# Two edits to a one-core block kernel: a halved update in a triangular inverse, and a reordered start of a recurrence

## The reference

```
a_low = where(strict, beta * (k k^T) * decay, 0)
sol = triangular_solve(a_low + eye, [v * beta, k * beta * exp(G)])
```

```
u = u + mu[0] * (prev - u) + mu[1] * (nxt - u)
S = S * w + (S (-kk)) (kk * a)^T + v k^T;   y = S r
```

## Time and profile before

| | |
|---|---|
| median of 3 runs | 3051.03 us (3050.25 to 3051.47) |
| profiled execution, its own time | 3045.2 us |
| its span | 3043.4 us |
| PE busy | 97% of the span |
| DVE / ACT / POOL busy | 49% / 36% / 8% |
| mean granted PE clock | 0.992 |

### The profile page before, as it was taken

The page is one execution under the profiler, slowest core; times in us unless marked ns, Lnnn a source line. Parts: engine busy times, 40 slices in busy tenths (PEclk is TensorE's granted clock), DMA queues, the critical chain, the costliest instruction groups (busy, mean ns, idle before and its releaser), DMA issues.

```text
span 3043.4 us, 46816 instructions
## 1 busy us (share of the span) xinstructions
PE 2942.6 (97%) x21214; PEld 2427.2 (80%) x21214; DVE 1479.4 (49%) x1443; ACT 1092.8 (36%) x1186; POOL 234.0 (8%) x135
## 2 busy tenths in 40 slices
PE   8998899999999999999999999999999998999998
PEld 6777778888888788888878878788878887888886
DVE  6765553444355444443454444555675654644432
ACT  5554442222345832222342222442244432332222
POOL 1002110000100010000110000320001220000001
PEclk9999999999999999999999999999998999999999
DMA  3210022222322012223222223312230002222231
GB/s 142 83 60 2 2 83 97 97 97 107 108 86 92 33 70 97 97 97 108 106 83 97 97 98 110 105 63 83 81 109 5 3 5 115 88 93 97 96 110 69
DMA packets 44902, 249.29 MB, mean 82 GB/s; under 512 B 8444, under 2 KB 12284, under 8 KB 17185
## 3 DMA queue, kind: packets, MB, share of 16 engines
q1 hardware_dynamic: 43552, 242.11, 22.4%
q10 hardware_dynamic: 1152, 4.19, 0.3%
HBM read 237.90 MB, written 8.39 MB: 81 GB/s over the span
## 4 chain that ended last, share of the span: by engine, by line
PE 85%; DVE 8%; ACT 4%; issue 2%; POOL 1%; DMA 0%; SPq 0%; DVEq 0%; ACTq 0%; POOLq 0%
PE ps L588 68%; PE ps L2756 7%; PE ps L1407 2%; ACT whi L266 1%; PE ps L2344 1%; DVE wlo L272 1%; PE ps L2328 1%; DVE gdn_XX L1775 1%; PE ps L3800 1%; PE ps L3781 1%; PE ps L3812 0%; PE ps L2064 0%; PE ps L2943 0%; DVE rw_u L1041 0%; DVE gdn_conv L1041 0%
## 5 line engine op out<-in xcount | busy, mean ns | idle before, releaser
L272 DVE TENSOR_TENSOR wlo<-wraw,whi 128x2048 fp32r<-128x2048 f32 x210 | 486.5, 2317 | 940.4 <-ACT whi L266 940.3
L266 ACT ACTIVATE whi<-wraw 128x2048 fp32r<-128x2048 f32 x210 | 402.1, 1915 | 926.6 <-PE ps L588 926.5
L588 PE MATMUL ps<-ffn_xh,whi 128*128 128x512 f32 x1408 | 552.3, 392 | 3.6 <-DVE ffn_xl L389 2.1
L588 PE MATMUL ps<-ffn_xh,wlo 128*128 128x512 f32 x1408 | 551.7, 392 | 0.0
L588 PE MATMUL ps<-ffn_xl,whi 128*128 128x512 f32 x1408 | 548.2, 389 | 0.0
L588 PEld LDWEIGHTS ps<-ffn_xh,whi 128*128 128x128 f32 x1408 | 264.5, 188 | 60.6 <-DVE ffn_xl L389 2.5
L588 PEld LDWEIGHTS ps<-ffn_xl,whi 128*128 128x128 f32 x1408 | 264.3, 188 | 59.4 <-issue 0.7
L588 PEld LDWEIGHTS ps<-ffn_xh,wlo 128*128 128x128 f32 x1408 | 264.4, 188 | 57.6
L588 PE MATMUL ps<-ffn_uh,whi 128*128 128x512 f32 x704 | 276.5, 393 | 0.0
L588 PE MATMUL ps<-ffn_uh,wlo 128*128 128x512 f32 x704 | 275.5, 391 | 0.0
L588 PE MATMUL ps<-ffn_ul,whi 128*128 128x512 f32 x704 | 273.5, 388 | 0.0
(11 more groups left out here) (509 smaller groups left out, 4705.5 us busy)
## 6 DMA issues: line engine op xcount, KB each, us to landing
wraw<-in_weights SPq DMA_DIRECT2D x211, 1024.0 KB, 4.8
gates_kept<-gates_tmp ACTq DMA_DIRECT2D x8, 512.0 KB, 4.1
mix_gate<-gates_kept SPq DMA_DIRECT2D x8, 512.0 KB, 10.8
h<-in_x SPq DMA_DIRECT2D x4, 512.0 KB, 9.5
mix_y<-hz_kept SPq DMA_DIRECT2D x2, 1024.0 KB, 6.3
out<-out SPq DMA_DIRECT2D x4, 512.0 KB, 3.2
wraw<-in_weights SPq DMA_DIRECT2D x2, 512.0 KB, 7.9
ple_raw<-in_p SPq DMA_DIRECT2D x4, 256.0 KB, 5.1
```

The source lines that it names most:

```text
L266: c.nc.scalar.activation(c.whi[:, j % 2, :], c.wraw[:, j % 2, :], ACT.Copy).then_inc(c.hi_ready, 1)
L272: c.nc.vector.tensor_tensor(c.wlo[:, j % 2, :], c.wraw[:, j % 2, :], c.whi[:, j % 2, :].bitcast(F32), ALU.subtract).then_inc(c.lo_ready, 1)
L588: last = nc.tensor.matmul(pair[:, m, :], a, b, start=opens and n == 0 and wa + xa == 0, stop=closes and n == len(ks) - 1 and wa == 1)
```

## The change

1. **Halved update.** `pe_right` signals `Z0` behind the X half and `Z` behind the XT half. `dve_right` is two subtractions of 128x512 in place of one of 128x1024: X behind `Z0` (signal `X`), XT behind `Z` (signal `XX`). The next `pe_left` waits for `X`, the next `pe_right` for `XX`. `Y21` still waits for `XX`.
2. **Preparations ahead of the last eviction.** DVE's slots 17 to 28 of the first preparation go behind tile 6 in place of tile 7, so ahead of the last `pad`.
3. **Late taps of two tiles.** Tiles 6 and 7 both leave their DVE taps for later, and these run in stage 0 of the recurrence in slots 21, 23, 25 and 27, one tap (two instructions) in each, in place of slot 5.
4. **Other banks.** The recurrence's banks depend on the projection's last pair: here Y = 6, Z = (0, 1), F = (4, 5), A = 2, C = 3. PE waits at the start for the `pad` of tile 6 alone, and for that of tile 7 only ahead of stage 1.

```diff
-            self.V.plan([f"{self.name}.pad{q}"] + [f"{self.name}.tap{q}.{w}" for w in range(1, len(self.taps))])
+            self.V.plan([f"{self.name}.pad{q}"])
+            for of in (q,) if q < n - self.late else range(n - self.late, n) if q == n - 1 else ():
+                self.V.plan([f"{self.name}.tap{of}.{w}" for w in range(1, len(self.taps))])
...
-        if not (self.late and r == len(self.body) - 1):
-            self.dve_taps(dve, q)
+        if q < len(self.body) - self.late:
+            for w in range(1, len(self.taps)):
+                self.dve_tap(dve, q, w)
...
         if l:
-            pe.wait_ge(*self.at("XX", i - 1))
+            pe.wait_ge(*self.at("X", i - 1))
...
         if l == 0:
             pe.wait_ge(*self.at("attT", 2 * k + 1))
+        else:
+            pe.wait_ge(*self.at("XX", i - 1))
         for h in range(2):
             for n in range(NC):
-                self.both(lambda r: X[r, h * NC + n, :], lambda r: self.XX[r, 1, h, n, :], lambda r: self.Y[r, h, n, :])
+                last = self.both(lambda r: X[r, h * NC + n, :], lambda r: self.XX[r, 1, h, n, :], lambda r: self.Y[r, h, n, :])
+        last.then_inc(*self.done("Z0"))
...
-        dve.wait_ge(*self.at("Z", LV * k + l))
-        XX = self.XX[:, :, :, :, :].rearrange("p x h n t -> p x (h n t)")
-        self.c.nc.vector.tensor_tensor(XX, XX, self.bank(self.Z_BANK, 2), ALU.subtract).then_inc(*self.done("XX"))
+        for x, (made, done) in enumerate((("Z0", "X"), ("Z", "XX"))):
+            dve.wait_ge(*self.at(made, LV * k + l))
+            X = self.XX[:, x, :, :, :].rearrange("p h n t -> p (h n t)")
+            self.c.nc.vector.tensor_tensor(X, X, self.bank(self.Z_BANK + x), ALU.subtract).then_inc(*self.done(done))
...
-    Y_BANK, Z_BANK, F_BANK, A_BANK, C_BANK, MISC = 0, (1, 2), (3, 4), 5, 6, 7
+    BANKS = ((6, (2, 3), (4, 5), 0, 1, 7), (6, (0, 1), (4, 5), 2, 3, 7))
...
-        pe.wait_ge(*self.shift.free(len(RW_ORDER) - 1))
+        last = len(RW_ORDER) - 1
+        pe.wait_ge(*self.shift.free(last - 1))
         for k, build, step, prepare, finish in self.pairs():
+            if k == 1:
+                pe.wait_ge(*self.shift.free(last))
...
-        for s in {3: range(8), 4: range(8, 12), 5: range(12, 17), 7: range(17, SLOTS)}.get(r, ()):
+        for s in {3: range(8), 4: range(8, 12), 5: range(12, 17), 6: range(17, SLOTS)}.get(r, ()):
...
-                if k == 0 and s == 5:
-                    self.shift.dve_taps(dve, len(RW_ORDER) - 1)
+                if k == 0 and s in (21, 23, 25, 27):
+                    of, w = divmod((s - 21) // 2, 2)
+                    self.shift.dve_tap(dve, len(RW_ORDER) - 2 + of, 1 + w)
```

More of the change, by code:

```diff
@@ L959, in __init__ @@
     def __init__(self, c, name, n, norm, dst, padded, taps, pad, bias=None, func=None, conv=None, beside=(),
-                 beside_pe=(), held=0, first=True, dst_free=None, order=None, late=False):
+                 beside_pe=(), held=0, first=True, dst_free=None, order=None, late=0):
         self.late = late
@@ L1024, in dve_evac, with dve_tap @@
                                 ALU.mult).then_inc(*self.V.done(f"{name}.pad{q}"))
-        if not (self.late and r == len(self.body) - 1):
-            self.dve_taps(dve, q)
+        if q < len(self.body) - self.late:
+            for w in range(1, len(self.taps)):
+                self.dve_tap(dve, q, w)
         for b in self.beside:
             b.vector_beside(dve, r)
-    def dve_taps(self, dve, q):
+    def dve_tap(self, dve, q, w):
         nc, name = self.c.nc, self.name
[L1032 to L1043, removed]
+        if w == 1:
+            dve.wait_ge(*self.V.at(f"{name}.pad{q}"))
+            dve.wait_ge(*self.A.at(f"{name}.tap{q}"))
+        else:
+            dve.wait_ge(*self.V.at(f"{name}.tap{q}.{w - 1}"))
+        at, col = self.taps[w]
+        for m in range(2):
+            to = self.to(q, m)
+            last = nc.vector.scalar_tensor_tensor(to, self.padded[:, q % 2, m, at:at + T], col(2 * self.order[q] + m), to,
+                                                  ALU.mult, ALU.add)
+        last.then_inc(*self.V.done(f"{name}.tap{q}.{w}"))
 def vec_at(c, name):
@@ L1282, in __init__ @@
         self.sems, self.made = {}, {}
-        for engine, cycles in (("pe", ("rb", "rq", "rg", "kk tX Y21 X12", "qk", "Y", "Z", "tv", "tk", "kS", "vn", "dS", "o",
+        for engine, cycles in (("pe", ("rb", "rq", "rg", "kk tX Y21 X12", "qk", "Y", "Z0 Z", "tv", "tk", "kS", "vn", "dS", "o",
                                        "osum")),
                                ("act", ("eg", "Dx", "vT", "kdT", "Xc Y21c Xd X12c", "Yc", "VN", "oc osq", "oln", "ors hi")),
-                               ("dve", ("eye", "kb", "qn", "diff", "dm qd", "AT", "off XT0", "attT", "XX", "R", "S", "on og lo", "zero")),
+                               ("dve", ("eye", "kb", "qn", "diff", "dm qd", "AT", "off XT0", "attT", "X XX", "R", "S", "on og lo", "zero")),
                                ("pool", ("CT", "mc"))):
@@ L2560, in __init__ @@
         self.j_held = c.tile
+        self.Y_BANK, self.Z_BANK, self.F_BANK, self.A_BANK, self.C_BANK, self.MISC = self.BANKS[(c.groups - 1) % 2]
         put = lambda name, shape, at: c.at(f"rw_{name}", shape, at)
@@ L4065, in second_half @@
     shift = Taps(c, "rw_u", 8, norm, u, padded, taps, 1, held=2, first=False, dst_free=keep.free,
-                 order=RW_ORDER, late=True)
+                 order=RW_ORDER, late=2)
     shift.beside_sync = (keep,)
```

## The result

| | before | after |
|---|---|---|
| median of 4 runs beside each other | 3051.25 us (3050.25 to 3051.82) | 3026.4 us (3025.8 to 3027.51) |
| ratio, 95% interval | | 0.9932 [0.9919, 0.9945] |
| span of the profiled execution | 3043.4 us | 3024.8 us |
| mean granted PE clock in it | 0.992 | 0.994 |

The medians differ by 24.9 us, the two spans by 18.6 us. The ratio, taken at the 3051.0 us of the forecast, is 3030.3 us [3026.3, 3034.2]; the forecast was 3032 us.

A forecast was written before the change was run, and what follows sets the result against it. PE, busy 97% of the span, was taken as the bound, so only its idle and slow time could be won. 8.2 + 0.3 + 1.3 - 0.5 + 10.0 = 19.3 us off 3051.0 gave 3032 us; 8-in-10 range 3027 to 3043.

The forecast's parts named there:

- the clean one: Likeliest case: all terms arrive and the clock does not fall at the recurrence; 3032 us, own range 3028 to 3036, chance 0.50.
- Halved update: Delta rule's core, four stages: PE's waits for the subtraction shrink, winning 8.2 us, bounds 4 and 11.8.
- the losses that I charged for the fuller DVE: Delta rule's later stages: DVE's extra instruction loses waits of 1.4 and 0.33 us and adds 0.15 to 0.2 us.
- The start of the recurrence: Recurrence's start: PE no longer waits for the last pad, but LT limits the win to 0.3 us, bounds 0 and 1.7.
- the 1.7 us that PE wins come out as 0.2 to 0.35 us: Recurrence's start: POOL's mask product and DVE's L3178 wait for LT, which starts little earlier; 0.3 us taken.
- Taps out of slot 5: Recurrence's first right product: `ys` is ready ahead of need, so PE's idle time goes; 1.3 us won, bounds 1.0 and 1.3.
- Late taps in slots 21 to 27: Recurrence's stage 0: taps fit DVE's room, but a POOL mask product may overrun slot 21; 0.5 us charged, bounds 0 and 3.
- The clock: Recurrence from about 2297 us: with less PE idle time the stretch at 1.2 GHz goes, winning 10.0 us.
- The slow stretch stays: Rival, recurrence: the clock falls at 2297 all the same, so only 9.3 us are won; 3042 us, chance 0.20.
- The early fall: Rival, recurrence's start: the clock falls at about 2279 for 3 to 5 us; 3036 us, chance 0.18.
- The other side: Rival, recurrence: an early fall lasts, costing up to 14 us more; 3056 us, chance 0.05 shared with some wait unseen.
- The halves do nothing: Rival, delta rule: POOL's mask product or PE's order bounds left products, 2 to 4 us won; 3037 to 3047 us, chance 0.07.

The follow-up runs named there:

- e1: Kernel before with only the halved update of Inverse added, recurrence untouched: 3038.84 us, before beside it 3047.84 us.
- e8: Kernel after, unchanged, run again in a later set: 3029.94 us, before beside it 3047.78 us, ratio 0.9943.
- e12: Kernel after, unchanged, run a third time for comparison: 3027.33 us, before beside it 3050.1 us, ratio 0.9927.
- e10: Kernel after with the preparations of slots 17 and later back behind the last eviction: 3029.22 us, before beside it 3050.1 us.
- e6: Kernel before with only the recurrence's other banks and its first build waiting for the last but one pad: 3051.59 us, before beside it 3047.78 us.
- e3: Kernel before with only tile 7's late taps moved from slot 5 to slots 25 and 27: 3036.71 us, before beside it 3047.84 us.
- e5: Kernel before, taps still in slot 5, with unread PE products filling the wait for `ys`: 3038.01 us, before beside it 3047.78 us.
- e4: Kernel after with the taps where before had them, tile 6's in the projection, tile 7's in slot 5: 3042.12 us, before beside it 3047.84 us.
- e7: Kernel before with only the preparations of slots 17 and later put ahead of the last eviction: 3053.21 us, before beside it 3047.78 us.

## Why the prediction was right, and where its sizes were off

1. **The case was the likeliest, the clean one.** By the ratio after is at 3030.3 us, inside the range and inside the likeliest case's own 3028 to 3036; its bare median, 3026.4, is just below both. Its later ratios, 0.9943 and 0.9927, are 3033.6 and 3028.7 us. The mechanism was right: the halves, the wait behind the taps, the clock. But part of the hit is luck. Four terms were too small, by 3.4 us together, and a loss elsewhere that I had not priced (4.4 us in the profiled execution) made up for it; and the clean case needed a step that I had wrong (3).
2. **Halved update: 8.2 us forecast, 9.6 measured up to the last Y21, 8.3 up to the output's products behind it.** From the first kk product (215.50 before, 216.43 after) and then from Y21 to Y21 (250.54, 289.44, 331.34, 370.95 before; 247.72, 284.65, 324.84, 362.31 after) the four stages win 3.8, 2.0, 1.7 and 2.1 us; forecast 3.4, 1.6, 1.3 and 1.9. In the last three stages the losses that I charged for the fuller DVE (waits of 1.4 and 0.33 us lost, 0.15 to 0.2 us on top) came in part only. What I had not seen is the longer wait for ACT's copy of Y behind the last Y21, and that the clock can fall at the two waits in the third stage (2.7 us in e1, e8 and e12). The terms as written add to 8.1, since the second and third stage's are rounded up.
3. **The start of the recurrence: 0.3 forecast, 1.2 measured** (first values product at 11.3 us behind the start of the last matmul before, 10.1 after). Pad and LT came as worked out, 1.6 us later (forecast 1.7) and 0.4 us earlier (0.2 to 0.35). The step that failed is "the 1.7 us that PE wins come out as 0.2 to 0.35 us": it took L3178's 1.75 us as a fixed duration. It was the price of coming second to POOL. 1.06 us fall away there, and a wait of 0.75 for MQ, in place of 0.28, takes 0.5 us of it again. I had cited the rule for the late taps and not applied it to the row in front of me. The error was on the lucky side twice. With 1.75 us there, as forecast, PE would have idled 0.95 and some 2 us; e10 has just this, 0.82 and 1.96, and there and in e6 the clock fell.
4. **Taps out of slot 5: 1.3 forecast, 1.5 measured**, from left(0, 1) to the right product, start to start (2.45 us before, 0.95 after). The row's 1.30 us of idle time is counted from a modelled end; starts are the better measure. The wait isn't the taps alone, either. They push DVE's scan behind POOL's mask product, and it takes 2.29 us in place of the 1.22 of e3 and of after. Before, and then e3:
```profile
2291.96 1.34 POOL L2715 TENSOR_TENSOR rw_CT<-rw_LT,rw_mask 128x512 f32<-128x512 f32 x1 [8.68 <-PE ps L2756]
2292.09 2.29 DVE L3236 TENSOR_TENSOR_SCAN rw_t<-rw_resets,rw_t 128x512 f32<-128x512 f32 x1
```
```profile
2289.58 1.22 DVE L3236 TENSOR_TENSOR_SCAN rw_t<-rw_resets,rw_t 128x512 f32<-128x512 f32 x1
```
By these rows 1.07 of the 1.30 us are that: an estimate, as no run has the taps in slot 5 without POOL beside the scan.
5. **Late taps in slots 21 to 27: 0.5 charged, nothing seen.** They ran in DVE's gaps, took 1.40 or 1.41 us each, so none was held up by POOL, and the pairs of products kept their 2.99 us.
6. **The clock: 10.0 forecast.** 13.1 less 1.2 and 1.5 leaves 10.4 us for this and the line above, and before's 42.18 against the 31.78 and 31.77 of e3 and e5 gives the same. (The forecast's own terms add to 16.5 us at full clock and so to 9.9; after takes 16.0, from 2289.19 to 2305.20.) e3, e4 and e5 show the mechanism from three sides.
7. **The edits of the start are worth something only together**, which the sum didn't say. Up to the first values product, banks alone or preparations alone lose 1.1 and 5.6 us (e6, e7), both with tile 6's taps still in the projection lose 2.0 (e4), banks and late taps without the preparations win nothing (e10), and all three win 1.2.
8. **The 5.8 us between before's profiled execution and its median** can be clock as well: over all sets before's runs lie between 3036.9 and 3058.6 us with mean clocks of 0.996 down to 0.988, and span times clock is 3020. So 24.9 us by the medians of four runs holds some luck; the later medians differ by 17.8 and 22.8 us, around the 19.3 forecast.
9. **The rivals.** The slow stretch stays: refuted, no trace of after has it. The early fall: it did not come in after, whose two waits there are 0.6 and 0.7 us and not the two long ones I had feared. But it is real: e6 and e10 have it behind waits of 1.0 or 0.8 and 1.96 us, e4 and e7 behind 3.8 and 6.3. It was short in all four, and in e6 and e10 it cost 1.1 us where I had said 4. *The other side*, an early fall that lasts, was seen in no trace. The halves do nothing: refuted by e1. What I had not priced is the loss right behind the last Y21 and new short falls elsewhere, which together take back 4.4 us of what the delta rule wins: 9.6 + 1.2 + 1.5 + 10.4 is 22.7 us, less 4.4 is 18.3, and the spans differ by 18.6.

## What to carry to other kernels

Look at the granted clock behind every idle time of the tensor engine: here 1.3 us of waiting cost 10 us more behind it, and moving four VectorE instructions to gaps some 20 us later was worth as much as all the rest of the change. A duration in a profile may hold another engine's: before it enters a sum, see what ran beside it and who started first. Reorderings of one start belong in one experiment, since each alone can lose what all together win, and a filler's own wait must not be later than the one that it fills.

## What was not expected of the hardware

- The clock stays at 1.2 GHz through dense work: from 2297 to about 2321 us before, with PE busy 3.00 of 3.00 us in every window but one (2.43 in 2303 to 2306), and so in e4 and in e6 (0.66 still in 2325 to 2328); in e1's profiled execution the same place was back at 1.00 after some 7 us. What ends it early wasn't found. The Trainium skill, "TensorE: Matmul & The Clock Gate", section "What's actually happening", lets activity release the throttle; these rows show 24 us of it without a release, mostly in products of 64x64 and 64x32. The last window before the clock came back:
```profile
2318.00:2321.00 3.00, 3.00 (x64) 3.00 (x60) 2.29 (x5) 0.06 (x1) 0.01 (x1) 0.50 0.00 0
```
- Whether an idle time of 1 to 3 us is followed by a fall differs between executions of one kernel. After, e8 and e12 are the same kernel: the third stage of the delta rule has the fall in e8's and e12's traces and not in after's, and 1540 to 1560 us has it in after's alone. What decides it wasn't found. With it go a spread of 22 us between before's runs, and of 5.5 us between after's.
